# Moving the low operand parts and half of the gathered tokens by 64 bytes inside SBUF

## The reference

```python
def swiglu(h, w_gate, w_up, w_down):
    return (jax.nn.silu(h @ w_gate) * (h @ w_up)) @ w_down

# first network: layer 0 = attention/recurrence mixer, then a dense swiglu (1024 -> 2816 -> 1024)
#                layer 1 = gated delta net, then a mixture of experts:
def moe_swiglu(h, router, w_gate, w_up, w_down):
    logits = (t @ router).astype(jnp.float32)
    top_v, top_i = lax.top_k(logits, TOP_K)              # 2 of 8 experts for each token
    ...
    for e in range(N_EXPERTS):
        y_e = swiglu(t, w_gate[e], w_up[e], w_down[e])   # 1024 -> 3584 -> 1024
        out = out + gates[:, e:e + 1] * y_e
# second network, two layers: swiglu (2816), a convolution / gating mixer, swiglu (2816)
```

## Time and profile before

| | |
|---|---|
| median of 3 runs | 2405.79 us (2405.57 to 2406.63) |
| span of the profiled execution | 2403.7 us |
| TensorE busy (matmul) | 2382.4 us, 99% |
| weight loads (beside matmuls) | 2017.0 us, 84% |
| VectorE, ScalarE busy | 1872.4 us (78%), 1438.0 us (60%) |
| granted TensorE clock, mean | 0.999 |
| HBM | 252 GB/s over the span |

### The profile page before, as it was taken

How to read it: one execution, slowest core, us unless ns; L and a number is a source line. 1 busy time by engine, 2 the same in 40 slices (tenths; PEclk the granted TensorE clock), 3 DMA queues, 4 the chain that set the end, 5 groups by cost and what they waited for, 6 DMA issues and landing times.

```text
span 2403.7 us, 34175 instructions
## 1 busy us (share of the span) xinstructions
PE 2382.4 (99%) x12542; PEld 2017.0 (84%) x12542; DVE 1872.4 (78%) x1961; ACT 1438.0 (60%) x1474; POOL 14.2 (1%) x34
## 2 busy tenths in 40 slices
PE   8999999999999999999999999999999999999998
PEld 7788899888888888888888888888788888897887
DVE  7767786678888888888888898677966676688666
ACT  6645455567777777777777776555254454544444
POOL 1000000000000000000000010000000000000000
PEclk9999999999999999999999999999999999999999
DMA  8375143459999999999999996853355566533653
GB/s 301 116 251 177 68 147 130 146 207 376 380 377 348 374 379 378 348 377 377 377 348 373 381 395 246 278 177 123 132 193 175 194 227 230 176 126 123 200 191 125
DMA packets 315952, 603.73 MB, mean 251 GB/s; under 512 B 9120, under 2 KB 135200, under 8 KB 315552
## 3 DMA queue, kind: packets, MB, share of 16 engines
q1 hardware_dynamic: 314160, 592.70, 69.1%
q10 hardware_dynamic: 1136, 7.87, 0.8%
q0 software_dynamic: 576, 2.10, 0.2%
HBM read 597.91 MB, written 8.91 MB: 252 GB/s over the span
## 4 chain that ended last, share of the span: by engine, by line
PE 94%; DVE 2%; ACT 1%; DMA 1%; DVEq 1%; issue 0%; SPq 0%; ACTq 0%
PE bank L205 20%; PE bank L206 20%; PE bank L207 19%; PE bank L1218 17%; PE bank L1222 9%; PE bank L3513 1%; PE bank L2955 1%; PE bank L3440 1%; PE bank L2230 1%; PE bank L2240 1%; DMA mslot<-in_e_w_in 1%; PE bank L2930 1%; PE bank L1714 1%; PE bank L1058 0%; PE bank L2149 0%; PE bank L2249 0%
## 5 line engine op out<-in xcount | busy, mean ns | idle before, releaser
L3205 DVE TENSOR_TENSOR weights_lo<-mslot,weights_hi 128x2048 fp32r<-128x2048 f32 x336 | 767.5, 2291 | 117.5 <-ACT weights_hi L3098 116.5
L3098 ACT ACTIVATE weights_hi<-mslot 128x2048 fp32r<-128x2048 f32 x336 | 644.0, 1919 | 217.4 <-PE bank L207 214.2
L1370 DVE TENSOR_TENSOR weights_lo<-scratch,weights_hi 128x2048 fp32r<-128x2048 f32 x165 | 377.2, 2289 | 166.3 <-ACT weights_hi L1363 166.2
L1218 PE MATMUL bank<-x_parts,weights_hi 128*128 128x512 f32 x1760 | 441.2, 392 | 1.8 <-DVE x_parts L921 1.8
L1218 PEld LDWEIGHTS bank<-x_parts,weights_hi 128*128 128x128 f32 x1760 | 319.4, 189 | 63.8 <-DVE x_parts L921 2.4
L205 PE MATMUL bank<-weights_hi,x_pair 128*128 128x512 f32 x896 | 356.9, 398 | 0.2 <-issue 0.2
L206 PE MATMUL bank<-weights_lo,x_pair 128*128 128x512 f32 x896 | 351.4, 392 | 0.0
L207 PE MATMUL bank<-weights_hi,x_pair 128*128 128x512 f32 x896 | 349.9, 391 | 0.0
L1363 ACT ACTIVATE weights_hi<-scratch 128x2048 fp32r<-128x2048 f32 x165 | 315.3, 1914 | 49.3 <-PE bank L207 49.0
L205 PE MATMUL bank<-weights_hi,hidden_hi 128*128 128x512 f32 x808 | 315.9, 391 | 0.0
L206 PE MATMUL bank<-weights_lo,hidden_hi 128*128 128x512 f32 x808 | 315.2, 390 | 0.0
(11 more groups left out here) (561 smaller groups left out, 2735.0 us busy)
## 6 DMA issues: line engine op xcount, KB each, us to landing
mslot<-in_o_moe_w_gate SPq DMA_DIRECT2D x112, 1024.0 KB, 6.8
mslot<-in_o_moe_w_up SPq DMA_DIRECT2D x112, 1024.0 KB, 6.8
mslot<-in_o_moe_w_down SPq DMA_DIRECT2D x112, 1024.0 KB, 6.9
scratch<-in_ffn_w_gate SPq DMA_DIRECT2D x44, 1024.0 KB, 5.2
scratch<-in_ffn_w_up SPq DMA_DIRECT2D x44, 1024.0 KB, 5.1
scratch<-in_ffn_w_down SPq DMA_DIRECT2D x44, 1024.0 KB, 5.0
mslot<-in_o_w_in SPq DMA_DIRECT2D x7, 2048.0 KB, 10.8
scratch<-in_e_ffn_w_gate SPq DMA_DIRECT2D x11, 1024.0 KB, 5.2
```

Of the source, the lines that this page charges most:

```text
L1218: pe.matmul(m.ps[bank + j][:, :], hi[:, k, cols(j)], both, start=(k == 0), stop=False)
L1370: dve.tensor_tensor(m.wlo[to][:, :], m.fslot[i], m.whi[to][:, :], ALU.subtract).then_inc(m.sig["f_lo"], 1)
L3098: act.activation(m.whi[(place + half) % PLACES][:, :], r.slot[slot + half], ACT.Copy).then_inc(s["r_hi"], 1)
L3205: dve.tensor_tensor(m.wlo[i][:, :], r.slot[slot + half], m.whi[i][:, :], ALU.subtract).then_inc(s["r_lo"], 1)
```

## The change

Tiles of 64 bytes (`PHASE` = 16 floats) are put between the allocations, which moves `weights_lo`, `hidden_lo` and the high half of `x_pair` by 64 bytes modulo 128. What shares memory with them is shifted to fit: the tiles of the gated delta net that lie in `scratch` move by 128 bytes, and `mixT`, which lies where `weights_lo2` lies, by 64. One operand that was named through `x_pair` is now named through `scratch_parts`, at the same byte (220,736). Every engine has the same instructions in the same order with the same waits as before.

```diff
+PHASE = 16
@@ place
     m.whi = [sb(f"weights_hi{i}", PIECE, F32R) for i in range(3)]
+    sb("phase0", PHASE)
     m.wlo = [sb(f"weights_lo{i}", PIECE, F32R) for i in range(3)]
+    sb("phase1", PHASE)
     m.x2 = cut(sb("x_parts", KT * 2 * SEQ, F32R), 0, KT, 2, SEQ)
-    m.hh, m.hl = sb("hidden_hi", HALF, F32R), sb("hidden_lo", HALF, F32R)
+    m.hh = sb("hidden_hi", HALF, F32R)
+    sb("phase2", PHASE)
+    m.hl = sb("hidden_lo", HALF, F32R)
...
-    m.xg = cut(sb("x_pair", 2 * PIECE, F32R), 0, 2, KT, 2 * P)
+    sb("phase3", PHASE)
+    xg = sb("x_pair", 2 * PIECE + PHASE, F32R)
+    m.xg = [cut(xg, i * (PIECE + PHASE), KT, 2 * P) for i in range(2)]
@@ odd_out_piece
-        hi = m.xg.rearrange("p i k t -> p (i k t)")[:, PIECE - 48:2 * PIECE - 48] if half == 0 else \
+        hi = m.scr_parts(21504, PIECE) if half == 0 else \
@@ odd_mem: BV, Y, S, tmp, KD, qdT, sg, sq
-    o.KD = m.scr(18432, GH, P)
+    o.KD = m.scr(18432 + 2 * PHASE, GH, P)
@@ moe_mem
-    r.xg = [m.xg[:, i] for i in range(2)]
+    r.xg = m.xg
@@ the second network's mixer
-    c.mixT = m.scr(10240, KT, SEQ)
+    c.mixT = m.scr(10240 + PHASE, KT, SEQ)
```

More of the change, by code:

```diff
@@ L185, in place @@
     m.whi = [sb(f"weights_hi{i}", PIECE, F32R) for i in range(3)]
+    sb("phase0", PHASE)
     m.wlo = [sb(f"weights_lo{i}", PIECE, F32R) for i in range(3)]
+    sb("phase1", PHASE)
     m.x2 = cut(sb("x_parts", KT * 2 * SEQ, F32R), 0, KT, 2, SEQ)
     m.xh, m.xl = m.x2[:, :, 0, :], m.x2[:, :, 1, :]
-    m.hh, m.hl = sb("hidden_hi", HALF, F32R), sb("hidden_lo", HALF, F32R)
-    with nc.sbuf_tensor("mixer_lows", [P, f0 + 3 * PIECE - 6 * PIECE - KT * 2 * SEQ - 2 * HALF], F32R) as lows:
-        m.c_low = [cut(lows, f0 - 6 * PIECE - KT * 2 * SEQ - 2 * HALF + i * KT * DC, KT, DC) for i in range(2)]
-    sb("scratch_rest", f0 + PIECE - 6 * PIECE - KT * 2 * SEQ - 2 * HALF)
-    m.xg = cut(sb("x_pair", 2 * PIECE, F32R), 0, 2, KT, 2 * P)
+    m.hh = sb("hidden_hi", HALF, F32R)
+    sb("phase2", PHASE)
+    m.hl = sb("hidden_lo", HALF, F32R)
+    free = f0 - 6 * PIECE - KT * 2 * SEQ - 2 * HALF - 3 * PHASE
+    with nc.sbuf_tensor("mixer_lows", [P, free + 3 * PIECE], F32R) as lows:
+        m.c_low = [cut(lows, free + i * KT * DC, KT, DC) for i in range(2)]
+    sb("scratch_rest", free + PIECE)
+    sb("phase3", PHASE)
+    xg = sb("x_pair", 2 * PIECE + PHASE, F32R)
+    m.xg = [cut(xg, i * (PIECE + PHASE), KT, 2 * P) for i in range(2)]
     return m
@@ L2013, in odd_mem @@
     pair = lambda at: [m.scr(at + t * 1024, GH, P) for t in range(NT)]
-    o.dec, o.LT, o.T, o.TT, o.BV = pair(6144), pair(8192), pair(10240), pair(12288), pair(16384)
+    o.dec, o.LT, o.T, o.TT, o.BV = pair(6144), pair(8192), pair(10240), pair(12288), pair(16384 + 2 * PHASE)
     o.AT, o.U = o.dec, o.LT
-    o.Y = [m.scr(14336 + a * 512, 4, P) for a in range(2 * NT)]
-    o.S, o.tmp = pair(14336)
-    o.KD = m.scr(18432, GH, P)
+    o.Y = [m.scr(14336 + 2 * PHASE + a * 512, 4, P) for a in range(2 * NT)]
+    o.S, o.tmp = pair(14336 + 2 * PHASE)
+    o.KD = m.scr(18432 + 2 * PHASE, GH, P)
     o.gb = [o.KD, o.T[0]]
-    o.qdT = m.scr(19456, GH, P)
+    o.qdT = m.scr(19456 + 2 * PHASE, GH, P)
     first = SMALL_COLS["w_a"][0]
-    o.sg = [m.scr(20480, D), m.small[:, first:first + D]]
+    o.sg = [m.scr(20480 + 2 * PHASE, D), m.small[:, first:first + D]]
     o.o = m.scr(2048, NT, GH, P)
-    o.sq = m.scr(21504, GH, SEQ)
+    o.sq = m.scr(21504 + 2 * PHASE, GH, SEQ)
     o.xh, o.xl = m.odd_x2[:, :, 0, :], m.odd_x2[:, :, 1, :]
```

## The result

The changed kernel takes 2424.32 us (median of 5 runs, 2423.88 to 2424.77), the kernel before, run on the same chip, 2406.08 us (2405.57 to 2406.63). The ratio is 1.0075, with a 95% interval of 1.0064 to 1.0086: slower by 18.2 us where 2397 was forecast, and above the end of the range, 2413.

The account below looks back on a forecast made before the run. TensorE was taken as the bound, the time being the sum of distances between the starts of 12,542 matmuls. Terms -9 + 0 + 1.3 - 0.8 = -8.5 us took the median from 2405.8 to 2397.3 us, range 2387 to 2413.

Parts of the forecast that it names:

- step 7: ScalarE, VectorE and DMA queues: shifted operands cost 0, since idle time would hide up to 13%.
- signs of being wrong: Triples over 230.6 ns, narrow groups settling at 118 ns, or TensorE beginning to wait for `weights_lo` in the experts.
- Step 1: 220 narrow groups of 8 matmuls: `weights_lo` at 0 makes them cheaper, -9 us taken between -10.2 and -2.4.
- step 5: 192 c-block matmuls: stationary operands all at 0 save 4.3 ns each, -0.8 us.
- Step 2: Experts' gate and up, 2688 matmuls: like pairs give 227.8 ns, -3.2 us, bounds -6.7 and +7.5.
- Step 3: Down, 2424 matmuls: same pattern of like pairs, 227.8 ns, +3.2 us, bounds 0 and +12.8.
- Step 4: Last chunks with hidden parts in `x_parts`, 80 triples: low weights at 0 cost 5.3 ns per matmul, +1.3 us.
- Step 6: 1760 wide matmuls: both operands stay at 64, term 0, with +-6 us for other neighbours.
- Rival C: Triples: mixed halves are dearer, down's moving weights step twice and never settle; 231.8 ns, +11.8 us, 2417.6 us, chance 0.22.
- Rival D: All matmuls: places are indifferent, differences come from PSUM banks or neighbours' lengths; 2405.8 us, chance 0.05.

Follow-up runs that it names:

- Run 1: Changed kernel with pads reordered so every tile is in its old half of 128 bytes, tiles from `x_parts` on still 128 bytes further; 2425.8 us, ratio 1.0081.
- run 5: Kernel before with everything from `scratch` on (weights, tokens, hidden parts, gathered tokens) moved together by 128 bytes; 2407.8 us, ratio 1.0006.
- run 8: Kernel before with token and hidden parts 256 bytes further from the weights and `x_pair` 64 bytes after its old place; 2402.0 us, ratio 0.9982.
- run 9: Against run 8, only the low weight parts moved, 64 bytes on; 2422.4 us, ratio 1.0067 to the kernel before.
- Run 12: Against run 9, the low half of `x_pair` also moved 64 bytes on, as in the change; 2420.5 us, ratio 1.0059 to the kernel before.
- run 7: Kernel before with `x_pair` moved 192 bytes down to the weights' place modulo 512, with the buffers that hang on it; 2402.0 us, ratio 0.9982.
- run 15: Kernel before with tokens 128 bytes on, hidden parts 256 bytes on and `x_pair` at distance 0 from the weights modulo 256; 2408.1 us, ratio 1.0006.
- run 6: Kernel before with only the hidden parts, stationary in the down products, moved by 128 bytes against the weights; 2418.3 us, ratio 1.0051.
- run 13: Kernel before with only the hidden parts moved, by 64 bytes against the weights; 2419.7 us, ratio 1.0055.

## Why the prediction was wrong

What held: TensorE's distances are the time, no engine and no transfer got into the way, the clock stayed, and so did ScalarE's 1919 ns and VectorE's 2291 ns (step 7). The sum of the classes is the difference of the spans. The matmuls' own durations did move with their distances, by -4 to +3 ns in the mean. Two of the prediction's own signs of being wrong came true: the triples cost over 230.6 ns, and narrow stands near 118 ns (118.7).

What failed first is the premise ahead of the steps, that the extra of a matmul "depends on the halves of 128 bytes in which moving and stationary operand begin". Run 1 keeps every half and loses 19.7 us; runs 5 and 8 lose nothing of the kind. What counts at 512 columns is how the tiles of the products lie to each other modulo 256 bytes. Before, the weights, the tokens and the hidden parts all lay at 64 modulo 256, and for the 512-column products this is the best arrangement found. A table modulo 128 could not show that the pads shift `x_parts`, `hidden_hi` and the low half of `x_pair` by 128 bytes.

- *Step 1, narrow*: direction right, size wrong. -3.7 us with 128 of step 5's c-block products, where -9 and -0.8 were taken. Of the two bounds the poor one held, 118.7 ns in the mean and near the 117.8 of the earlier trace rows; the same moving tile was no reason to take 113.3. By the place in the group, the second to the seventh distance fall from 120 to 117 ns and the eighth from 130 to 127, but the first rises from 117 to 122. The gain comes of the low weights (run 9, -3.1 us).
- *Step 2, the experts' triples*: -3.2 us was taken and +4.4 measured. The base of 229 ns was sound for a running chain (229.5 without the distances over 300 ns, 231.2 after). The reason given was that load and moving operand would pair "always alike". Run 12 has just that, and 233.1 ns; run 9, with unlike pairs, has 233.8. Likeness in pairs buys 0.7 ns. The low distances were found only where all tiles of a triple lie at one place modulo 256, as in run 7.
- *Step 3, down*: the largest miss of a term, +10.9 where +3.2 was taken, for the same reason as in step 2. Either of two departures is enough: 128 bytes at the hidden parts (run 6, 232.7 ns) or 64 at the low weights (run 9, 232.5). The changed kernel has both and 232.5, so they don't add. A likely reason, not shown, is that either one keeps the chains from settling.
- *Step 4*: +1.3 forecast, and +1.4 measured for all products with the tokens loaded, but this is luck: the 128 bytes, which the step didn't know of, alone give more (run 15, 236.2 ns against 235.0 after).
- *Step 6, wide*: "Both operands stay at 64" and a term of 0, with 6 us either way for other neighbours; measured +4.7. It was not the neighbours, or little: run 15 gives 233.5 ns from the 128 bytes at the tokens alone, run 12 only 231.1 with the low weights and `x_pair` moved.

Rival C came nearest. The arrangement that it names, moving weights that step to and fro, is dear: runs 9 and 12 have it without the 128 bytes and stand at 2422.4 and 2420.5. But the step is not needed, since runs 1 and 6 have none and down at 232.7 ns, and no run shows that it is the step that costs in run 9. C had +2.8 ns for an experts' product and +5.3 for a down one, and the means rose by 1.7 and 4.5, so its +20.3 us for both kinds are 5 too many. What carries the result beyond C's 2417.6 are the wide group (+4.7), which it left at 0, the narrow one, 6.1 us short of its gain, and 1.4 us in other products: 11.8 - 5.0 + 4.7 + 6.1 + 1.4 = 19.0. Rival D, that places are indifferent, is refuted by run 6. Leaving the 128 bytes out would most likely not have saved the change: run 12, which has all the intended moves but that of `hidden_lo`, is 14.4 us over before. The full set without the 128 bytes was not run.

Run 7 is the version that beats both: `x_pair` moves, with the buffers that hang on it, 2402.0 us, ratio 0.9982. It is a small gain, 4.3 us, whose interval (0.9973 to 0.9991) lies below 1. Whether narrow's 3 us can be had on top, with low parts of the dense gate and up apart from those of the experts, was not tried.

What stays open is the mechanism beneath. It would have to say why a tile 64 bytes after the others' place is dear whether it is the stationary or the moving one (233.7 and 232.5 ns), and cheap 64 bytes before it (229.4 and 229.6), and why at 256 columns one place for all is not the best. One rival the trace of run 6 speaks against, that the writes of the moved tile disturb TensorE: in the experts the hidden parts are written while gate and up products run, and these stay at 231.3 ns, while the down products, which read the parts, go up by 4.7.

## What to carry to other kernels

Before tiles are padded, write down the first byte of every operand pair of the hot products, modulo 256 and not only 128, together with all that lies behind the pad, since a pad moves that too. One badly placed operand in a triple can cost nearly as much as all three (down 232.5 ns in run 9, 233.7 in run 13), so test one tile at a time, with the rest held at one place, before two moves are joined. And a price read from a long, uniform chain is not that of groups of 8 between others.

## What the chip showed that was not expected

- Where operand tiles begin relative to each other, modulo 256 bytes, changes the distance of 512-column products by up to 6 ns. With the hidden parts alone moved: 228.0 ns at 0, 233.7 at 64, 232.7 at 128, 229.4 at 192. With the low weights alone moved: 227.8, 232.5, 232.3, 229.6. All from the weights on by 128 bytes together: no change in these classes (run 5).
- Moving either the loaded or the moving operand can do it, and the loads run beside the matmuls (2016.4 us of loads beside 2401.2 us of matmuls). The Trainium skill, "SBUF — State Buffer", section "SBUF: two separate sides", gives TensorE ports of its own that wait for no one. Run 6, in which only the loaded operand of the down products moves against their moving one and 11.4 us go into them, does not agree with a reading of it by which operand places are indifferent. Which access loses the time, no run here shows.
- A chain of the experts needs up to ten products to settle after a start, and the experts' mean stays 3 ns above the settled 226.7 ns even with all operands at one place (run 7). Of these 3 ns, 2.4 are the 66 distances of over 300 ns.
